# A hybrid trunk layer on one core: weight splits and block scaling taken from GpSimd to ScalarE and VectorE around the output product and the first MLP pair

## What is computed

```python
h = modulate(x, norm1_w, sh1, sc1)              # rmsnorm(x) * (1 + sc) + sh
proj = h @ w_in                                 # 20 tiles of 128 columns here
mix = concatenate([y_gla, y_conv, y_pool]) @ w_out
x = x + g1 * mix
h2 = modulate(x, norm2_w, sh2, sc2)
x = x + g2 * (square(relu(h2 @ w_mlp1)) @ w_mlp2)   # width 4096 inside
return rmsnorm(x, final_norm_w)
```

## Time and profile before

| | |
|---|---|
| median of 3 runs | 1137.13 us (1137.06 to 1140.05) |
| the profiled execution | 1135.82 us |
| its span | 1134.0 us |
| busy: PE, DVE, ACT, POOL | 1088.8, 832.8, 508.7, 333.3 us |
| granted TensorE clock, mean | 0.99 |
| input product, up to | 368 us |
| output product | 368 to 466 us |
| plain pair of the MLP | 470 to 501 us |
| further pairs, line 1302 | 501 to 804 us |

### The profile page before, as it was taken

The page is one execution under the profiler, slowest core; times in us unless marked ns, Lnnn a source line. Parts: engine busy times, 40 slices in busy tenths (PEclk is TensorE's granted clock), DMA queues, the critical chain, the costliest instruction groups (busy, mean ns, idle before and its releaser), DMA issues.

```text
span 1134.0 us, 15381 instructions
## 1 busy us (share of the span) xinstructions
PE 1088.8 (96%) x5056; PEld 864.6 (76%) x5056; DVE 832.8 (73%) x1068; ACT 508.7 (45%) x823; POOL 333.3 (29%) x295
## 2 busy tenths in 40 slices
PE   8899999999999899897999999999899999999995
PEld 4478888877888688576788888888688888888883
DVE  3777869636544885799877777787977777777776
ACT  4646523355624222348666666666522222222234
POOL 1000006386201353432433232323422222222323
PEclk9999999999999999899999999999999999999998
DMA  9423241001013564204865757666837745854604
GB/s 372 197 94 111 82 142 38 27 30 38 20 38 130 224 232 156 74 1 152 331 261 223 275 222 269 229 248 256 307 137 314 282 176 209 333 227 185 254 1 149
DMA packets 58894, 199.71 MB, mean 176 GB/s; under 512 B 5600, under 2 KB 6880, under 8 KB 58336
## 3 DMA queue, kind: packets, MB, share of 16 engines
q1 hardware_dynamic: 58848, 199.11, 46.9%
HBM read 139.32 MB, written 59.77 MB: 176 GB/s over the span
## 4 chain that ended last, share of the span: by engine, by line
PE 50%; DVE 2%; ACT 0%; POOL 0%; issue 0%; DVEq 0%
PE ob L1302 13%; PE main L1343 13%; PE sm L1302 10%; PE sm L1343 8%; PE ob L1343 6%; DVE slot L2287 0%; DVE stage_last L2334 0%; POOL XR L909 0%; DVE stage L2334 0%; DVE XR L2501 0%; DVE XR L2439 0%; DVE hid L2347 0%; DVE hid L2341 0%; DVE t_tmp L2327 0%; ACT rs L1869 0%
## 5 line engine op out<-in xcount | busy, mean ns | idle before, releaser
L1302 PE MATMUL ob<-h_sum,slot 128*128 128x512 f32 x540 | 131.8, 393 | 4.0 <-ACT hid L1749 3.0
L926 PE MATMUL main<-a_hi,w_hi 128*128 128x512 f32 x376 | 125.9, 416 | 2.6 <-DVE a_lo L2140 2.6
L1302 PEld LDWEIGHTS ob<-h_sum,slot 128*128 128x128 f32 x540 | 101.1, 188 | 28.4 <-issue 4.8
L1706 ACT ACTIVATE slot<-raw 128x512 fp32r<-128x512 f32 x80 | 50.4, 631 | 158.8 <-PE main L1343 77.4
L926 PE MATMUL main<-a_lo,w_hi 128*128 128x512 f32 x376 | 116.7, 392 | 0.0
L926 PE MATMUL main<-a_hi,w_lo 128*128 128x512 f32 x376 | 116.2, 390 | 0.0
L2439 DVE SCALAR_TENSOR_TENSOR XR<-main,mods,XR 128x512 f32<-128x512 f32 x112 | 83.3, 748 | 32.1 <-PE main L1343 30.3
L926 PEld LDWEIGHTS main<-a_hi,w_hi 128*128 128x128 f32 x376 | 66.7, 188 | 21.1 <-issue 5.8
L926 PEld LDWEIGHTS main<-a_hi,w_lo 128*128 128x128 f32 x376 | 70.6, 188 | 15.7
L926 PEld LDWEIGHTS main<-a_lo,w_hi 128*128 128x128 f32 x376 | 70.6, 188 | 15.7
L1302 PE MATMUL sm<-h_hi,slot 128*128 128x512 f32 x240 | 79.7, 393 | 0.5 <-ACT hid L1749 0.5
(11 more groups left out here) (334 smaller groups left out, 2494.7 us busy)
## 6 DMA issues: line engine op xcount, KB each, us to landing
hidden_kept<-stage SPq DMA_DIRECT2D x98, 512.0 KB, 4.4
raw<-wstream SPq DMA_DIRECT2D x60, 512.0 KB, 3.7
t_even<-hidden_kept SPq DMA_DIRECT2D x56, 512.0 KB, 5.6
raw<-wstream SPq DMA_DIRECT2D x16, 1024.0 KB, 5.6
stage<-hidden_kept SPq DMA_DIRECT2D x21, 512.0 KB, 5.3
stage_last<-hidden_kept SPq DMA_DIRECT2D x21, 512.0 KB, 6.0
wmod<-wm SPq DMA_DIRECT2D x4, 2048.0 KB, 23.2
mbuf<-wm SPq DMA_DIRECT2D x16, 512.0 KB, 3.8
```

Source lines behind the costliest of these rows:

```text
L926: ins = pe.matmul(main[:, bank, half * HALF:(half + 1) * HALF], w[:, slot, k, :], x[:, half * HALF:(half + 1) * HALF], start=begin, stop=end)
L1302: ins = pe.matmul(hid_bank(acc, odd), slots1[j][:, w, kp, :], parts[x][:, kp, :], start=PARTS[j][3] and kp == 0 and m == 0, stop=kp == KP ...
L1706: act.activation(slots2[j][:, 0, :, :, :], operand(s, j), ACT.Copy).then_inc(w2_hi, 1)
```

## The change

- POOL's instructions for T_OUT + 1, for the first two MLP tiles and for scaling blocks of xg are left out. T_OUT + 1 is copied by ACT after its last mix copy and subtracted by DVE after its last `low_mix`. The two MLP tiles are copied by ACT (`first_weights`) and subtracted by DVE (`weight_low`) between blocks of half 0. DVE scales all blocks.
- On DVE two `add_late` steps, not four, stand ahead of the first residual add; steps 2 and 3 come after it, before 4 and 5.
- On SP the load of T_OUT + 3 stands ahead of X's second half and of late loads 4 to 7.
- PE takes the plain pair in another order: four blocks of half 0 for tile 0, the square sum of the second half, the same four blocks for tile 1, then blocks 4 to 7 of half 0 and all of half 1 with both tiles in turn for each block.
- ACT makes the high parts of h2 in smaller groups between its squares, and the copy `sum_high(6)` stands ahead of `w1_high(1, 4)` and `first_hidden(0)` instead of behind them.

```diff
@@ sync
             for i in range(4):
                 load_late(i)
+            load_tile(T_OUT + 3)
             sp.dma_start(X[:, 4:8, :], ...).then_inc(x2_loaded[1], 16)
             for i in range(4, 8):
                 load_late(i)
-            load_tile(T_OUT + 3)
@@ gpsimd
-            for t in (T_OUT, T_OUT + 1):
-                pool.wait_ge(raw_loaded[t % 2], 16 * (t // 2 + 1))
-                pool.wait_ge(tile_done, stream_free(t - 2))
-                split(t % 2, t + 1, hi_made)
+            pool.wait_ge(raw_loaded[T_OUT % 2], 16 * (T_OUT // 2 + 1))
+            pool.wait_ge(tile_done, stream_free(T_OUT - 2))
+            split(T_OUT % 2, T_OUT + 1, hi_made)
+            pool.wait_ge(split_done, T_OUT + 2)
             ...
-            scale_blocks(0)
-            for b in range(2):
-                pool.wait_ge(raw_loaded[b], 16 * (T_MLP // 2 + 1))
-                pool.wait_ge(tile_done, stream_free(T_MLP + b - 2))
-                split(b, T_MLP + b + 1, hi_made)
-            scale_blocks(1)
@@ tensor
             for b in range(2):
                 pe.wait_ge(split_done, ready0 + b)
                 pe.wait_ge(main_free[1 - b], free0 + b)
-                direct(b, 0, None if b else lambda: squares_summed(acc2_made, 0, sums2_done, 1))
-            for b in range(2):
-                direct(b, 1).then_inc(hid_done, 1)
+                for n in range(KT // 2):
+                    hidden_block(0, b, n)
+                if b == 0:
+                    squares_summed(acc2_made, 0, sums2_done, 1)
+            for n in range(KT // 2, KT):
+                for b in range(2):
+                    hidden_block(0, b, n)
+            for n in range(KT):
+                for b in range(2):
+                    ins = hidden_block(1, b, n)
+                    if n == KT - 1:
+                        ins.then_inc(hid_done, 1)
@@ scalar
+            act.wait_ge(split_done, T_OUT + 1)
+            act.wait_ge(raw_loaded[(T_OUT + 1) % 2], 16 * ((T_OUT + 1) // 2 + 1))
+            act.wait_ge(tile_done, stream_free(T_OUT - 1))
+            act.activation(w_hi[:, (T_OUT + 1) % 2, :, :], raw[...], ACT.Copy).then_inc(hi_made, 1)
             ...
                 rsqrt(rs2[:, 0:HALF], sm[:, 0, :], D, rs_made)
+                before()
                 act.wait_ge(main_free[1], (m0 + KT - 2) // 2 + 1)
             ...
+            def first_weights(b):
+                act.wait_ge(raw_loaded[b], 16 * (T_MLP // 2 + 1))
+                act.wait_ge(tile_done, stream_free(T_MLP + b - 2))
+                act.activation(w_hi[:, b, :, :], raw[:, b, :, :], ACT.Copy).then_inc(hi_made, 1)
             ...
+            def first_highs():
+                act.wait_ge(mods_late, 1)
+                for k in H_ORDER[:2]:
+                    high(0, k)
+                first_weights(0)
             def early_highs():
-                act.wait_ge(mods_late, 1)
-                for k in H_ORDER[:5]:
+                for k in H_ORDER[2:4]:
                     high(0, k)
-            def late_highs():
-                for k in H_ORDER[5:]:
-                    high(0, k)
+                first_weights(1)
+            def late_high():
+                high(0, H_ORDER[4])
+            residual_squares(M_OUT, ..., first_highs, early_highs, late_high)
+            for k in H_ORDER[5:]:
+                high(0, k)
             ...
             sum_high(4)
+            sum_high(6)
             w1_high(1, 4, 1, True)
             ...
             first_hidden(0)
-            sum_high(6)
@@ vector
             for n in range(2, KT):
                 low_mix(n)
+            weight_low(T_OUT + 1)
             ...
-            for i in range(4):
-                add_late(i)
+            add_late(0)
+            add_late(1)
             ...
                         add(i, b)
-                        for n in range(2):
-                            add_late(4 + 4 * i + 2 * b + n)
+                        at = 4 * i + 2 * b + (2 if (i, b) == (0, 0) else 4)
+                        for n in range(at, 8 + 4 * i + 2 * b - 2):
+                            add_late(n)
             ...
-                for k in H2_DVE[0][:2]:
-                    scale(0, k)
+                scale(0, H_ORDER[0])
+                scale(0, H_ORDER[1])
+                low(0, 0)
             def next_blocks():
-                for n, k in enumerate(H2_DVE[0][2:5]):
-                    scale(0, k)
-                    low(0, n)
-                low(0, 3)
+                scale(0, H_ORDER[2])
+                low(0, 1)
+                weight_low(T_MLP)
+                scale(0, H_ORDER[3])
+                low(0, 2)
             residual(M_OUT, 0, acc2_made, sq2_made, 0, first_blocks, next_blocks)
-            for k in H2_DVE[0][5:]:
-                scale(0, k)
+            low(0, 3)
+            weight_low(T_MLP + 1)
             for n in range(4, KT):
-                low(0, n)
+                scale(0, H_ORDER[n])
+                if n > 4:
+                    low(0, n - 1)
+            low(0, KT - 1)
             dve.wait_ge(rs2_made, 2)
-            ...
+            for n, k in enumerate(H_ORDER):
+                scale(1, k)
+                if n >= 1:
+                    low(1, n - 1)
+            low(1, KT - 1)
```

More of the change, by code:

```diff
@@ L173 @@
 H_ORDER = (4, 5, 6, 7, 0, 1, 2, 3)
-H2_POOL = ((6,), (6, 0, 3))
-H2_DVE = tuple(tuple(k for k in H_ORDER if k not in H2_POOL[half]) for half in range(2))
 OUT_DVE = (5, 6)
@@ L433, in hybrid_trunk @@
         h2_scaled = sem("h2_scaled")
-        h2_scaled_pool = sem("h2_scaled_pool")
         xg_made = sem("xg_made")
@@ L835, in _ @@
             split_pairs(T_OUT // 2 + 1, T_MLP // 2)
-            def scale_blocks(half):
-                cols = slice(half * HALF, (half + 1) * HALF)
-                pool.wait_ge(rs2_made, half + 1)
-                for k in H2_POOL[half]:
-                    pool.wait_ge(xg_made, xg_count(k, half))
-                    pool.tensor_tensor(xg[:, half, k, :], xg[:, half, k, :], rs2[:, cols], ALU.mult).then_inc(h2_scaled_pool, 1)
-            scale_blocks(0)
-            for b in range(2):
-                pool.wait_ge(raw_loaded[b], 16 * (T_MLP // 2 + 1))
-                pool.wait_ge(tile_done, stream_free(T_MLP + b - 2))
-                split(b, T_MLP + b + 1, hi_made)
-            scale_blocks(1)
             def part_sums1(pair, b, first=False):
@@ L1255, in normed, with hidden_block @@
                 pe.wait_ge(lo_made, LO_H2 + half * KT + n + 1)
-            def direct(b, half, within=None):
-                for n, k in enumerate(H_ORDER):
-                    normed(half, n)
-                    if within is not None and n == 3:
-                        within()
-                    h, l = h_hi[half][:, k, :], h_lo[half][:, k, :]
-                    for w, x, begin, end in ((w_hi, h, n == 0, False), (w_hi, l, False, False),
-                                             (w_lo, h, False, n == KT - 1)):
-                        ins = pe.matmul(main[:, 1 - b, half * HALF:(half + 1) * HALF], w[:, b, k, :], x, start=begin, stop=end)
+            def hidden_block(half, b, n):
+                normed(half, n)
+                h, l = h_hi[half][:, H_ORDER[n], :], h_lo[half][:, H_ORDER[n], :]
+                for w, x, begin, end in ((w_hi, h, n == 0, False), (w_hi, l, False, False), (w_lo, h, False, n == KT - 1)):
+                    ins = pe.matmul(main[:, 1 - b, half * HALF:(half + 1) * HALF], w[:, b, H_ORDER[n], :], x, start=begin, stop=end)
                 return ins
@@ L1613, in _, with residual_squares @@
                 act.activation(shape(mix_parts(k)[0]), src, ACT.Copy).then_inc(mix_hi, 1)
-            def residual_squares(m0, acc_made, sq_made, nth, sums_done, rs_made, between, after):
+            act.wait_ge(split_done, T_OUT + 1)
+            act.wait_ge(raw_loaded[(T_OUT + 1) % 2], 16 * ((T_OUT + 1) // 2 + 1))
+            act.wait_ge(tile_done, stream_free(T_OUT - 1))
+            act.activation(w_hi[:, (T_OUT + 1) % 2, :, :], raw[:, (T_OUT + 1) % 2, :, :], ACT.Copy).then_inc(hi_made, 1)
+            def residual_squares(m0, acc_made, sq_made, nth, sums_done, rs_made, before, between, after):
                 def square(i, b):
@@ L2179, in _, with residual @@
             dve.memset(macc_late[:, :, :], 0.0).then_inc(late_cleared, 1)
-            for i in range(4):
-                add_late(i)
-            def residual(m0, g, acc_made, sq_made, nth, between, after):
+            add_late(0)
+            add_late(1)
+            def residual(m0, g, acc_made, sq_made, nth, before, between):
                 dve.memset(acc2[:, :], 0.0).then_inc(acc_made, 1)
@@ L2219, in residual @@
                 add_half(KT - 1, 0, res_half)
-                between()
+                before()
                 dve.wait_ge(tile_done, m0 + KT - 1)
                 add_half(KT - 2, 1, main_free[1])
+                between()
                 sum_half(1)
-                after()
```

13 lines of the change are left out of this document (2 added, 11 removed).

## The result

| | before | after |
|---|---|---|
| median | 1137.62 us (4 runs, 1137.06 to 1140.05) | 1129.28 us (4 runs, 1127.53 to 1130.52) |
| profiled execution | 1135.82 us | 1128.82 us |
| its span | 1134.0 us | 1127.0 us |

The ratio is 0.9922, with an interval of 0.9908 to 0.9937: faster beyond the noise, though by under 1%, and by 8.3 us between the medians. The forecast was 1125.5 us and a gain of 11.6.

What follows compares the result with a forecast made beforehand. PE was busy 96% of the span, so only its idle or half-clocked stretches could be won: 4.6 + 5.5 + 1.5 = 11.6 us off 1135.82 makes 1124.2, a median of 1125.5; range 1121.5 to 1131.1.

Steps and rivals of the forecast that it cites:

- the forecast case: Whole kernel: a gain of 10 to 13 us, chance 0.48.
- less: Whole kernel: GpSimd's sums keep half 1's low parts slow and the second residual add is late; gain 4 to 10, chance 0.28.
- the thin covers: Output product: work hidden with little time in hand, thinnest 0.8 us at the second residual add; if exceeded, 3.6 us won.
- term one: Output product: the fifth tile stretch could start at 412.03 instead of 416.65; 4.6 us won.
- Tile 4's load ... lands by 405 at worst: Output product: load issued near 399.6, split in 5.8 us, wanted by PE at 412.0; no wait.
- Add done at 400.2 ... 0.8 us: Output product, second residual add: done at 400.2, PE wants that bank at 401.0, 0.8 us in hand.
- 1.5 blocks made in 5 us: Output product: DVE makes 1.5 late blocks in 5 us beside GpSimd's split of a tile.
- Term two: First MLP products: PE starts without a gap and DVE reaches its half sums sooner; 5.5 us, bounds 3.5 to 7.5.
- Term three: Between the MLP's first pairs: DVE no longer waits 1.99 us for ACT's copy of sum 6; 1.5 us, bounds 0 to 2.0.
- Only moved idleness: Stage from 494 to 535 held by ACT's queue or a load, so only 0 to 3.4 us remain; chance 0.06.
- More: First MLP products: GpSimd's sums run while DVE waits for ACT, half 1 runs clean; 14 us, 1123, chance 0.14.
- Slower, the clock: MLP's first pairs: waits before products 1 to 4 keep the clock low; 8 us lost, 1145, chance 0.04.

Runs made afterwards that it cites:

- pe_order_back: The changed kernel with PE's block order of the plain pair as before (bank by bank): 1127.24 us, ratio 0.9894 to the kernel before.
- pool_weights: The changed kernel with the split of the first two MLP weight tiles given back to GpSimd: 1136.84 us, ratio 0.9986 to the kernel before.
- pool_scale: The changed kernel with GpSimd scaling its four blocks again: 1129.94 us, ratio 0.992 to the kernel before.

## Why the prediction was right, and where its terms were off

The side, the range and the mechanism held. The size was 8.3 us, where the forecast case had 10 to 13: by its size the result lies in the case *less*. Of that case's mechanism the thin covers came true (1.4 us of term one), the slow first half of the MLP, to which it had given up 2.5 us, did not; most of what was missing came from outside the terms.

**Term one (4.6 foretold, 3.2 measured).** The mix's low parts and the first residual add came out as written: two stretches of 11.0. Two steps, both of them sizes, were wrong.
- "Tile 4's load ... lands by 405 at worst ...: nothing." On the clock of after (2.0 later) that is an issue at 401.6 and a landing by 407; it was issued 0.9 later than that, at 402.45, because it stands behind DVE's late steps, and it was 7 us among the late loads until GpSimd began. The forecast had allowed 5.4 us, though it had itself read 8 us for tile 3's load before. That cost 0.8 us of wait and the stretch 1.0. Moving the load brought the 1.0 back, in both profiles that have it moved. In pe_order_back, whose code for it is that of after, the load landed 1.3 us earlier, counted from the output product's first matmul, and PE didn't wait: it is a cover of nearly nothing, not a fixed price.
- "Add done at 400.2 ... 0.8 us" in hand: it ended at 403.25, where the shifted forecast was 402.2 and PE's need 403.0. "1.5 blocks made in 5 us" was too kind: two steps took 6.43, of which the split covered some 5.4 and let 1.2 through. The trace before had said as much: its split of tile 2 ended at 388.11, so of the 8.49 us 3.46, some 2.8 steps, lay behind it, and 1.2 steps in the 5 us beside it. The neighbour's price counted twice, once ahead of each add.

The stretch came out 0.28 us too long. The Trainium skill (SBUF — State Buffer, Who interferes with whom) calls the port pair that DVE and GpSimd share an exclusive lock, and says, of DVE's 2-port modes, that whichever of the two issues first has it for its whole instruction and the other is kept out. The trace agrees for DVE instructions with two inputs in SBUF, here (the add ended at 401.25 on the old clock, where the prediction's weighing gave some 401.2 and 0.3 us) and in pool_weights, where DVE has exactly one such instruction done for each of GpSimd's.

**Term two (5.5 foretold, 6.1 measured).** Right, and by its steps: PE without a gap at full clock, DVE held up once by ACT (1.3 foretold, 1.23), GpSimd's sums beside DVE. The prediction left open which part pays; pool_weights and pool_scale give it to the weight splits (7.8 us if they return) and not to the scaling (1.1) or to PE's order (0.1 alone, 0.3 undone).

**Term three (1.5 foretold, 1.1 measured).** DVE's gap of 1.99 went. What took part of it back was not ACT's queue but GpSimd's next weight sums, now beside DVE: 1.78 at 512.19 where 0.68 is the price alone.

**Rivals.** *Only moved idleness* falls: the stage behind kept its length but for the third term. *More* falls, since the sums ran into DVE's work and not into its wait. *Slower, the clock*: the mechanism is real and was put in the wrong place. Products 1 to 4 of the pair showed it once, as before (4.48 us at 505.34 behind a wait of 2.39). It struck the second pair's wait, which both kernels have.

**The starting point.** "The same time to the end" and an unchanged start were assumed from one profile. That profile of before was a favourable one, by luck: at 1135.82 us it is faster than each of the 44 other runs of that kernel (1136.38 to 1140.69). Its product behind the 3.05 us wait ran at full clock, its row of narrow matmuls too, and its output product began at 367.99, where the 13 other profiles lie from 368.11 to 370.26. Such places differ from execution to execution of the same code. They made 3.4 us of the 4.6 by which the profiled execution of after (1128.82) missed the 1124.2; the terms made the other 1.2. So DVE's first half sum stands at 487.01 and not near 484, and the row of 535.11 at 526.70 and not near 523.5: 2.0 us of either is the start. Over all its runs the kernel before lay near 1138, some 1 us above the median that the sum started from.

## What to carry to other kernels

Where two engines slow each other down, the work to move away is that which stands beside an engine on the critical path and ahead of what other queues wait for: here two weight splits on GpSimd cost 8 us, four scalings 1. After a load's release has been moved, give the next load in the same queue the same look, its issue and its landing under the traffic of that moment. And before a sum is made from one profile, look for the places where its clock was at full rate only by luck, and set their price apart.

## What the runs showed of the hardware that was not expected

- A wait of PE of about 3.1 us was followed by a slow product in 10 of 12 profiles and by a fast one in 2, with the same products: 4.50 to 5.46 us against 3.05. The waits don't tell them apart: 3.04 to 3.23 us in the ten, 3.05 and 3.19 in the two. So one profile doesn't say whether a wait of this length costs clock.
- The granted clock fell below 1.00 in or behind the row of 32 matmuls of one column (3.6 us at full clock), though PE wasn't idle, in 8 of 12 profiles (1.00 in the other four); it cost 0.6 to 3.0 us.
- What stands beside GpSimd isn't always slow. The residual add, whose first source lies in PSUM, takes 1.27 us inside GpSimd's row of 418.62, as it does alone (1.27 at 401.98). The late steps, which read both inputs from SBUF, take 3.2 beside GpSimd (6.43 / 2) and 1.24 without it (2.48 / 2, from 405.80). DVE's and GpSimd's timelines, after:

```profile
419.54 1.27 DVE L2197 SCALAR_TENSOR_TENSOR X<-main,mods,X 128x1024 f32<-128x1024 f32 x1
```

```profile
418.62 3.28 POOL L768 TENSOR_TENSOR w_lo<-raw,w_hi 128x1024 fp32r<-128x1024 f32 x1
```
